# Moving two modulation units and the clearing of the result rows in the first stage of a one-core block kernel

## What is computed

```
mod = silu(c) @ w_ada + b_ada                    # 6 x 1024 columns, w_ada is 1024 x 6144
sh1, sc1, gt1, sh2, sc2, gt2 = split(mod, 6)
u = rmsnorm(x, g) * (1 + sc1) + sh1
z = u @ w_in                                     # 1792 + 1304 + 2048 columns
zr, zn, zg = split(z)
y_r = rwkv7_time_mix(zr)                         # a recurrence over the tokens
y_n = nsa_mix(zn)                                # compressed, selected and window attention
gates = sigmoid(zg)                              # two gates of 1024 columns each
merged = gates[0] * (y_r @ p_rwkv) + gates[1] * (y_n @ p_nsa)
h = x + gt1 * (merged @ w_out)
u2 = rmsnorm(h, g2) * (1 + sc2) + sh2
h = h + gt2 * moe(u2)                            # 32 experts, 2 per token
out = rmsnorm(h, g3)
```

## Time and profile before

| | |
|---|---|
| median of three executions | 1333.65 us |
| profiled execution, its own time | 1333.57 us |
| its span in the trace | 1331.8 us |
| TensorE busy | 1127.4 us, 85% |
| VectorE busy | 391.4 us, 29% |
| ScalarE, GpSimd busy | 219.5 us, 178.0 us |
| moved by DMA | 311.40 MB |

### The profile page before, as it was taken

How to read it: one execution, slowest core, us unless ns; L and a number is a source line. 1 busy time by engine, 2 the same in 40 slices (tenths; PEclk the granted TensorE clock), 3 DMA queues, 4 the chain that set the end, 5 groups by cost and what they waited for, 6 DMA issues and landing times. The chain is left out here.

```text
span 1331.8 us, 16841 instructions
## 1 busy us (share of the span) xinstructions
PE 1127.4 (85%) x7189; PEld 580.0 (44%) x7189; DVE 391.4 (29%) x670; ACT 219.5 (16%) x443; POOL 178.0 (13%) x236
## 2 busy tenths in 40 slices
PE   6999999599997887989799991988887878887880
PEld 5543444354555555979644451333332323332330
DVE  3334527332005354345522326111001010101004
ACT  4011224020003452334200120000000000000002
POOL 2100002033001343323100001001000000000003
PEclk7899999689997998999999995998998899989995
DMA  9512639934414000000082536799999999999965
GB/s 363 189 64 94 221 125 350 413 129 126 138 52 135 0 2 25 4 2 4 9 313 86 230 132 240 316 425 428 427 426 427 426 427 428 427 425 428 427 269 199
DMA packets 60323, 311.40 MB, mean 234 GB/s; under 512 B 8354, under 2 KB 14852, under 8 KB 46680
## 3 DMA queue, kind: packets, MB, share of 16 engines
q1 hardware_dynamic: 46792, 273.80, 51.3%
q0 software_dynamic: 11152, 32.32, 6.3%
q10 hardware_dynamic: 2304, 4.20, 0.8%
HBM read 284.60 MB, written 33.03 MB: 238 GB/s over the span
## 5 line engine op out<-in xcount | busy, mean ns | idle before, releaser
L2375 PE MATMUL ps<-ring,zrT 128*64 128x512 f32 x704 | 164.3, 622 | 23.8 <-issue 20.8
L963 PE MATMUL ps<-ring,uT 128*128 128x512 f32 x384 | 169.3, 598 | 1.2 <-PE ps L963 0.6
L2395 PE MATMUL ps<-ring,hdT 128*64 128x512 f32 x352 | 128.3, 669 | 10.8 <-issue 9.9
L954 PE MATMUL ps<-uT,ring 128*128 128x512 f32 x256 | 114.4, 604 | 2.0 <-DVE uT L687 1.4
L963 PEld LDWEIGHTS ps<-ring,uT 128*128 128x128 f32 x384 | 72.2, 191 | 92.8 <-issue 92.8
L2375 PEld LDWEIGHTS ps<-ring,zrT 128*64 128x64 f32 x704 | 56.9, 143 | 122.3 <-issue 121.9
L2200 DVE TENSOR_TENSOR zrT<-zrT,ps 128x512 f32<-128x512 f32 x16 | 11.0, 688 | 276.7 <-PE ps L2375 276.7
L2375 PE MATMUL ps<-mg,zrT 128*64 128x512 f32 x160 | 75.3, 626 | 7.7 <-issue 7.7
L2021 ACT ACTIVATE zrT<-ps 128x512 f32<-128x512 f32 x16 | 9.6, 597 | 414.4 <-PE ps L2375 414.4
L954 PEld LDWEIGHTS ps<-uT,ring 128*128 128x128 f32 x256 | 48.6, 193 | 67.0 <-issue 66.0
L1950 POOL DMA_INDIRECT y_dram<-zrT,y_at x16 | 16.2, 1015 | 430.2 <-DVE zrT L2209 430.2
(11 more groups left out here) (380 smaller groups left out, 1493.1 us busy)
## 6 DMA issues: line engine op xcount, KB each, us to landing
ring<-in_moe_w_gate_dram SPq DMA_DIRECT2D x22, 2048.0 KB, 30.1
ring<-in_moe_w_up_dram SPq DMA_DIRECT2D x22, 2048.0 KB, 32.8
ring<-in_moe_w_down_dram SPq DMA_DIRECT2D x22, 2048.0 KB, 33.3
ring<-in_w_in_dram SPq DMA_DIRECT2D x8, 2048.0 KB, 14.5
ring<-in_w_ada_dram SPq DMA_DIRECT2D x8, 2048.0 KB, 10.2
y_dram<-vrep POOLq DMA_DIRECT2D x1, 15872.0 KB, 58.1
mod<-in_moe_w_up_dram SPq DMA_DIRECT2D x5, 2048.0 KB, 32.6
mg<-in_moe_w_up_dram SPq DMA_DIRECT2D x5, 2048.0 KB, 31.6
```

Source lines behind the costliest of these rows:

```text
L954: ins = pe.matmul(ps[:, n % 4, :], slot(name, KD, w)[:, k, c0:c0 + P], uT[:, k, :], start=(k == 0), stop=(k == KD - 1))
L963: ins = pe.matmul(ps[:, n % 4, :], uT[:, k, P * i:P * i + P], w, start=(k == 0), stop=(k == KD - 1))
L2375: ins = pe.matmul(ps[HALF * r:HALF * r + HALF, "gu".index(kind), :], xgT[:, b % 2, k, HALF * r:HALF * r + HALF], w[r][:, k, :], start=(k = ...
L2395: ins = pe.matmul(ps[HALF * r:HALF * r + HALF, 2 + c, :], hdT[:, j, HALF * r:HALF * r + HALF], w[r][:, j, 512 * c:512 * c + 512], start=(j ...
```

## The change

The list of units becomes ..., kv, ada9, zg00, ada10, zg10, ada11, zg01, zg11, w1k, w1v: ada10 and ada11 now stand singly between gate units. Every ada unit is summed one tile later than the distance in the list gives: ada4 to ada9 at tiles 5, 9, 13, 15, 19 and 21 (spread after 7, 11, 15, 17, 21 and 23), ada10 at tile 29 (spread after 31), ada11 at tile 33 (spread after 35). The clearing of y_dram moves on GpSimd from behind round 0 to behind the ropes.

```diff
@@ stream_units
     win_unit("kv", NSA0 + 768, 512)
-    for u in (9, 10, 11):
-        ada_unit(u)
-    for j in range(2):
-        for b in range(2):
-            win_unit(f"zg{b}{j}", GATE0 + D * b + 512 * j, 512)
+    ada_unit(9)
+    for n in range(4):
+        j, b = n // 2, n % 2
+        win_unit(f"zg{b}{j}", GATE0 + D * b + 512 * j, 512)
+        if n < 2:
+            ada_unit(10 + n)
@@ build
-        ada_at, u = [], 4
+        ada_at, u, now = [], 4, 0
         for _, name, _, _ in ztiles:
             ada_at.append([])
-            while u < 12 and index[f"ada{u}"] < (index[name] if name else NU) + RP - 1:
+            now = index[name] if name else now
+            while u < 12 and index[f"ada{u}"] < now + RP - 1:
                 ada_at[-1].append(u)
                 u += 1
+        ada_at = [[]] + ada_at[:-1]
         ada_later = [[], []] + ada_at[:-2]
-        ada_later[-1] = ada_later[-1] + ada_at[-2] + ada_at[-1]
@@ gpsimd
                     pool.tensor_tensor(bt[:, c, :], av[:, :], eis[c % 2][:, :], ALU.mult).then_inc(w_b, 1)
-                    if c == 0:
-                        pool.wait_ge(c_v0, 2)
-                        pool.dma_start(y_dram.rearrange("(p b) (a d) -> p (b a) d", p=P, a=2),
-                                       vrep[:, :].unsqueeze(1).to_broadcast([P, 2 * NBLK, 512]))\
-                            .then_inc(c_fill, 16)
...
                         link(pool.tensor_tensor(kh[:, :, 1, :], th[:, :, 1, :], sh[:, :, 0, :], ALU.add))
+                pool.wait_ge(c_v0, 2)
+                pool.dma_start(y_dram.rearrange("(p b) (a d) -> p (b a) d", p=P, a=2),
+                               vrep[:, :].unsqueeze(1).to_broadcast([P, 2 * NBLK, 512])).then_inc(c_fill, 16)
                 pool.wait_ge(w_b, CT)
```

## The result

The changed kernel takes 1342.2 us (1339.36 to 1342.94, 4 executions) against 1333.79 before: the ratio is 1.0056, with a 95% interval of 1.0044 to 1.0068, so it is slower by 8.4 us. The profiled execution took 1339.36 us, its span is 1337.6; the other three took 2.7 to 3.6 us longer.

A forecast was written before the change was run, and what follows sets the result against it. The prediction took TensorE, busy 85% of the span, as the bound, with a 13.81 us stall in stage 1. Its terms, -17.0 + 13.1 + 6.3 + 2.0 = +4.4 us on 1333.57, gave 1338.0, range 1325 to 1343.

The forecast's parts named there:

- Sign, mechanism and range: Whole kernel: slower by 4.4 us, through K0's wait for w1k and the half clock behind it; range 1325 to 1343.
- (a) the stall: Gl tiles in stage 1: ada10 and ada11 leave them, so TensorE's stall before the second spread goes, -13.8 us.
- (b) the spreads: Spreads of ada10 and ada11: they move behind tiles 31 and 35 and run at full instead of half clock, -4.0 us.
- (c): Gl tiles and tile 28: the clock still falls, and tile 28 follows sooner and loses more, +0.8 us.
- term -17.0: TensorE up to tile 39: stall gone, spreads faster, some clock lost; -17.0 us, bounds -14 and -21.
- The wait for w1k: Before K0: w1k lands at 356.3 behind the clearing's bytes, so TensorE waits 13.1 us, bounds 0 and 17.
- The clock behind it: After the wait: K0 runs at half clock, +6.3 us, and tile 40 begins at half clock, +2.0 us.
- B: At K0: the wait is there but K0 wins the clock back; -1.9 us, 1331.7, chance 0.22.
- C: At K0: w1k comes in time, no wait, clock kept; -17.0 us, 1316.6, chance 0.15.
- D: At K0: a wait of only 5 to 9 us, clock still lost; between -4 and 0 us, chance 0.13.
- No price for the sums a tile later: Stage 1: summing ada4 to ada9 one tile later leaves TensorE as many spreads and costs nothing.

The follow-up runs named there:

- e12: Reordered units, sums where they were, clearing behind round 0, but ada9's spread on TensorE moved from after tile 22 to after tile 23; 1317.0 us.
- e7: The changed kernel with the clearing written in rows of half the length (256 floats); 1343.0 us.
- e8: The changed kernel with job K0 after tile 41 instead of after tile 39, all loads unchanged; 1318.9 us.
- e3: The changed kernel with a quarter of the clearing (16 of 62 pieces) issued behind round 0, the rest behind the ropes; 1332.8 us.
- e1: The changed kernel with the clearing of y_dram back behind round 0, units reordered and sums later as in the change; 1320.3 us.
- e5: The changed kernel with the clearing issued right behind the memset of vrep, at 36 us; 1319.8 us.
- e10: The changed kernel, clearing behind the ropes, with every unit summed at the tile of the kernel before; 1338.9 us.
- e6: The changed kernel with the clearing back behind round 0 and every unit summed at the tile of the kernel before; 1314.8 us.

## Why the prediction was right, and where not

- **Sign, mechanism and range held.** Forecast 1338.0 in 1325 to 1343, measured 1342.2, which is near the upper end. The forecast was +4.4 us, the medians give +8.4: the size was short by half.
- **(a) the stall, (b) the spreads.** The stall is gone; the spreads of ada10 and ada11 take 2.1 us each at full clock. As priced.
- **(c) and the term -17.0: this is the step that was mis-sized.** Tile 39 ended at 346.6, before at 360.15: -13.6, outside the term's own bounds of -14 and -21. Three things make up nearly all of the 3.4 us. The gl tiles took 13.9 us instead of 11.6 (+2.3): the step that failed is "the clock still falls in the gl tiles", which took for granted that it falls as late in them as before and costs nothing more. In the changed kernel it fell at their beginning. The spread of ada9 in front of them may be the reason (e12), but as e7 and e8 took 12.4 and 11.75 us in the same order, how much of the 2.3 belongs to it stays open. Tile 18 began 2.1 us later (189.67 against 187.54). Of this 1.2 are the start and the first four tiles, which vary from 29.1 to 30.8 us over the runs, whatever the edit; this part is chance. The other 0.9 are the three pauses that the later sums bring. Tile 28 took 7.68 us instead of 8.09, -0.4 where +0.8 stood.
- **The wait for w1k**, 13.1 expected, 13.32 measured. From tile 31's end (286.4) to w1k's landing 73.4 us passed; the sum of bytes had 73.0. (The clearing's 15.5 MB in the text and 16.25 in the sum are the same 15872 KB, in units of 1024 x 1024 and of a million bytes.) Some of that closeness is luck: the clearing was issued at 288.7 and not near 284, and the queues moved 28.76 MB in this stretch and not 27.8, with a ninth store of gates and the first 0.7 MB of w1v. e3 gives the slope, e1, e5 and e8 remove the wait.
- **The clock behind it.** K0 +6.6 (6.3 expected), the first zg11 tiles +1.4 (2.0). Not priced: the last job C1 (L909) was at half clock too, 1.94 us against 1.07.
- **Rivals.** B (K0 wins the clock back) falls: the granted clock was 0.50 through all of K0, as at the earlier trace rows; the sustained-activity rule of the Trainium skill, *TensorE: Matmul & The Clock Gate*, Part 1, would have given 6.3 us less, and the measurement decides against it for matmuls of 62 columns. C (w1k in time) falls with w1k's landing at 359.8; what the Trainium skill says in *DMA: Bandwidth & Descriptors*, Queues, rings and completion order, of queues taking turns by packet agrees with 163 to 162 packets. D (a shorter wait) falls: it was 13.32 us.
- **No price for the sums a tile later:** wrong. The medians of e1 and e6 differ by 5.5 us, those of the changed kernel and e10 by 3.3. In e1's stage 1, which ends 4.3 us after e6's, 2.8 are the gl tiles, 1.7 the tile behind job S0 and 0.9 the three pauses; e1's first four tiles happened to be 1.0 faster.

The sum by the measured terms, all from one trace of each kernel, is -13.6 + 13.3 + 6.6 + 1.4 + 0.9, less the 0.3 us gap that stood before K0 anyway: +8.3, against 8.26 at the end of stage 1.

The best version is e6: the reordered units, the sums where they were, the clearing behind round 0. It takes 1314.8 us, ratio 0.9854 (0.9834 to 0.9875). That e8's later K0 or e5's earlier clearing would add to it was not tried.

## What to carry to other kernels

Before moving a large transfer, add up all bytes of all queues between the first load that will stand beside it and the instruction that needs the last one, and compare that with the compute in the same stretch; the wait came out to 0.2 us here, in part by luck. A transfer whose end nobody awaits belongs where the queues are idle, and a job that does await one belongs behind work that needs nothing from the queue. Count a lost clock as part of a wait of some microseconds (4.1 us in e10, 4.2 in e3), and where a stretch of small matmuls loses the clock anyway, allow for the fall coming sooner or later from one trace to the next: 11.75 to 14.0 us in the same order here.

## What the runs showed that I had not expected

- The same 24-column matmuls in the same order took 11.75 to 14.0 us in the eight traces that have the changed kernel's order up to them, since the clock fell sooner in some and later in others. With a modulation spread moved one tile, to stand ahead of them, they took 13.7 us instead of 10.6 (e12 and e6, one trace each).
- Behind waits of 4.19 us (e3) and 4.13 us (e10) the granted clock was still 1.00 when K0 began, and it fell to 0.50 within K0's first microsecond or so; K0 took 13.65 and 13.18 us. Behind the changed kernel's 13.32 us it was at 0.50 from K0's start (13.89 us). K0 entered at full clock without a wait kept it (7.33).
- The clearing's packets were 4 KB whether its rows were 2 KB or 1 KB neighbours or 2 KB rows apart (3984, 3984 and 4000 packets for 16.25 MB).
